# A two-block transformer step on one Trainium2 core: queries and keys projected by tokens, normed along the free axis, and turned by TensorE

## The chip, the cores and the metric

The kernel runs on 1 core of one Trainium2 chip, in one launch. The metric is the device time in microseconds. The kernel before takes 1256.78 us, the median of 3 runs (1255.48 to 1257.05). The trace comes from one further execution, of 1257.0 us, whose span from the first to the last instruction is 1253.6 us.

## What is computed

256 tokens of width 1024 go through two blocks, in float32.

Block one norms `x` and projects it with `w_in` into nine groups of columns. Three branches follow: a gated depthwise convolution over 31 taps with a layer norm; a differential attention with 8 heads, each with two maps of 64 dimensions; and a cross attention with 4 heads of 256 dimensions against a memory of 256 tokens. Queries and keys of both attentions are RMS-normed per head:

```
q = rms_norm(q.reshape(B, S, H, 2, d), qn_g)      # differential, d = 64
k = rms_norm(k.reshape(B, S, H, 2, d), kn_g)
q = rms_norm(q.reshape(B, S, X_HEADS, X_HEAD_DIM), qn_g)   # cross, 256
k = rms_norm(k.reshape(B, M, X_HEADS, X_HEAD_DIM), kn_g)
```

The three results are gated by the `merge` columns, summed, projected with `w_out` and added to `x`.

Block two norms again and runs a stick-breaking attention (8 heads of 64, normed queries `q2` and keys `k2`) beside a gated linear recurrence `h_t = a_t h_{t-1} + b_t` (`a_t` from a softplus of a constant `rg_lambda`). Then a layer picks, for each token and each of 8 heads, 16 of 16384 experts (two rows of 1024 each), and sums their outputs.

## The kernel before

**Slots and pieces.** Every projection is cut into slots of 512 output columns; a slot is two pieces, each 1 MB of weights (128 partitions x 2048 floats) loaded by one DMA of the SP queue. ScalarE (ACT) rounds a piece to `w_hi` (`hi`, L885), VectorE (DVE) forms the rest `w_lo` (`lo`, L1505), and TensorE (PE) makes three products for each tile: hi x hi (L443), input lo x w hi (L444), input hi x w lo (L445). Two raw buffers and three pairs of hi and lo buffers go round, so `hi` of piece p waits until TensorE is through with piece p-3.

**Two orientations.** In a channel-major slot the weights are stationary and 256 tokens move past: 4 x 8 tiles, 96 products of 256 columns, and the result lies by channels. In a token-major slot the input is stationary and 512 weight columns move: 8 x 2 tiles, 48 products of 512 columns, and the result lies by tokens. Queries and keys of both blocks are channel-major, values and merge columns token-major.

**A head norm before.** `head_copy` (L964) copies the slot out of PSUM and squares it on ACT; `head_sums` (L483) multiplies the squares by ones on TensorE, after the next slot's products; `head_root` (L1018) does a logarithm and an exponential over the spread sums on ACT, each with a table load (L876), since the two tables differ; `head_scale` (L1625) multiplies on DVE. In block two, `q2` and `k2` are first scaled by the token's inverse norm on DVE (`scale_slot`, L1618), which also empties PSUM.

**The order.** Each engine's program is written out by hand, and runs in that order. The attention loop goes over 18 slots: q0 k0 v0 q1 k1 v1 xq0 xq1 xk0 xk1 xv0 xv1 m0 to m5. In step n TensorE projects slot n, does the head sums of slot n-1, then work of attention heads: values of head n-5, transposes of the probabilities of head n-4, scores of head n-3 (the cross heads follow eight steps later). In step n DVE does `lo` of the piece two ahead, some convolution taps, the probabilities of head n-4, the second `lo`, taps again, the head scale, and the row maxima of head n-3. Taps on DVE: 3 after each `lo` for n under 4, 2 for n under 12, then 4. GpSimd (POOL) does tiles 3 to 6 of the convolution, and the last 8 of the 31 taps of tile 7, after DVE has done the first 23.

**After the attentions** come the slots dg0 dg1 xg0 xg1 dp0 dp1 cg0 cg1 xp0 xp1 cp0 cp1 o0 o1. The mean of the convolution's layer norm (`conv_mean`) is multiplied before dp0, its variance after dp0; DVE takes a reciprocal of the root (L2085) and does two operations for each of the 8 tiles. Then block two: the slots xr, q2, k2, g2, v2. Ahead of q2, ACT issues five DMAs (L1375, L1380), loads a table and computes `exp(-|lambda|)` (L1384, L1386), and DVE computes constants of the recurrence from it in a chain of small operations (L2154 to L2175) before `lo` of q2. The stick-breaking logits follow (`sb_logits`), then L621 (`sb_weights`), the output products, and the choice of experts. From the first choice on, POOL issues indirect DMAs that fetch an expert's two rows for each token.

## Time and profile before

| what | value |
|---|---|
| median of 3 runs | 1256.78 us |
| the profiled execution | 1257.0 us, span 1253.6 us |
| TensorE busy | 1109.1 us (88%) |
| VectorE busy | 976.4 us (78%) |
| ScalarE busy | 565.6 us (45%) |
| GpSimd busy | 564.7 us (45%) |
| mean DMA rate | 299 GB/s over the span |
| granted TensorE clock | 0.990 of full speed on average |

Busy time counts overlapping instructions once. Matmuls are pipelined: one is on record for longer than the distance to the next one's start, so a busy share of 1 does not say how fast the products follow each other; that is read from start times. The first half of the span, to about 606 us, is the two blocks' dense work; from there on the experts' rows are fetched, at about 427 GB/s.

### The profile page before, as it was taken

The page shows a single profiled execution, that of the slowest core. Times are in us where ns is not written, and L with a number is a line of the kernel's source. Part 1 is how long each engine was busy: PE and PEld are TensorE (multiplying, and loading weights), DVE is VectorE, ACT ScalarE, POOL GpSimd, SP SyncE. Part 2 cuts the span into 40 slices and gives each one's busy share as a digit, 9 for nine tenths or more (in the row PEclk, how much of TensorE's full clock was granted, in tenths as well). Part 3 has the DMA queues.
Part 4 walks back from the last instruction along what each step waited for, and adds up shares of the span by engine and source line. Part 5 has one row for each costly group of instructions (what it writes and reads, how often), then busy time and mean ns, then how long its engine had stood idle before and what let it go on. Part 6 is the DMA issues. An engine that isn't in the chain of part 4 may idle for free.

```text
span 1253.6 us, 14289 instructions
## 1 busy us (share of the span) xinstructions
PE 1109.1 (88%) x5044; PEld 747.1 (60%) x5044; DVE 976.4 (78%) x1972; ACT 565.6 (45%) x1037; POOL 564.7 (45%) x539
## 2 busy tenths in 40 slices
PE   6999999999999998999588987988878897788777
PEld 6989798788999888977343432444324443232222
DVE  5569989998789767687898678886788868787755
ACT  5666768764456444796323333233332333222311
POOL 0099999998320000000444554544544445343432
PEclk9999999999999999999899999999999999999999
DMA  6544333344555554335799999999999999999996
GB/s 245 202 169 158 132 144 139 137 148 153 202 189 181 205 194 171 145 123 227 308 427 427 426 427 427 427 426 427 428 426 427 427 426 424 427 427 423 427 426 272
DMA packets 53943, 374.27 MB, mean 299 GB/s; under 512 B 6896, under 2 KB 6896, under 8 KB 9200
## 3 DMA queue, kind: packets, MB, share of 16 engines
q0 software_dynamic: 37152, 268.45, 50.9%
q1 hardware_dynamic: 14512, 100.67, 22.1%
q10 hardware_dynamic: 2208, 4.24, 1.0%
q8 instruction: 39, 0.64, 0.2%
q14 instruction: 32, 0.26, 0.1%
HBM read 372.29 MB, written 1.05 MB: 298 GB/s over the span
## 4 chain that ended last, share of the span: by engine, by line
PE 44%; DMA 26%; DVE 21%; ACT 5%; issue 3%; POOL 0%; ACTq 0%; POOLq 0%; DVEq 0%; SPq 0%
DMA big<-in_experts,big 11%; PE unit L443 10%; PE unit L444 10%; PE unit L445 10%; PE unit L760 8%; DMA row<-in_experts,big 5%; DMA conv_in<-in_experts,big 5%; DMA work_two<-in_experts,big 4%; DVE w_lo L1505 3%; DVE row L1959 2%; DVE big L1959 2%; DVE big L1865 2%; ACT L876 2%; DVE big L1862 2%; DMA w_raw<-in_weights 1%
## 5 line engine op out<-in xcount | busy, mean ns | idle before, releaser
L1229 ACT ACTIVATE probs<-ident,big 128x128 f32<-128x128 f32 x255 | 102.4, 402 | 430.3 <-DVE big L1969 430.3
L443 PE MATMUL unit<-in_hi,w_hi 128*128 128x256 f32 x800 | 263.3, 329 | 3.9 <-DVE w_lo L1505 3.4
L760 PE MATMUL unit<-row,probs 128*128 128x512 f32 x448 | 215.3, 610 | 44.1 <-ACT probs L1229 43.9
L1505 DVE TENSOR_TENSOR w_lo<-w_raw,w_hi 128x2048 fp32r<-128x2048 f32 x89 | 205.9, 2319 | 54.8 <-ACT w_hi L885 54.5
L444 PE MATMUL unit<-in_lo,w_hi 128*128 128x256 f32 x800 | 226.9, 284 | 0.0
L445 PE MATMUL unit<-in_hi,w_lo 128*128 128x256 f32 x800 | 226.7, 283 | 0.0
L885 ACT CAST w_hi<-w_raw 128x2048 fp32r<-128x2048 f32 x89 | 169.1, 1905 | 96.8 <-PE unit L445 53.4
L760 PE MATMUL unit<-big,probs 128*128 128x512 f32 x344 | 168.4, 619 | 43.6 <-ACT probs L1229 43.5
L2333 POOL DMA_INDIRECT row<-in_experts,big x112 | 133.6, 1193 | 129.0 <-PE unit L760 113.3
L760 PEld LDWEIGHTS unit<-row,probs 128*128 128x128 f32 x448 | 78.2, 190 | 153.9 <-ACT probs L1229 95.3
L443 PEld LDWEIGHTS unit<-in_hi,w_hi 128*128 128x128 f32 x800 | 154.1, 193 | 26.6 <-issue 20.9
L444 PEld LDWEIGHTS unit<-in_lo,w_hi 128*128 128x128 f32 x800 | 154.2, 193 | 20.7 <-issue 20.6
L1959 DVE CUSTOM_DVE_ANT_0 row<-big,row 128x1024 f32<-128x1024 f32 x112 | 136.5, 1219 | 37.9 <-DMA row<-in_experts,big 37.9
L2333 POOL DMA_INDIRECT big<-in_experts,big x85 | 100.7, 1185 | 123.0 <-PE unit L760 108.7
L445 PEld LDWEIGHTS unit<-in_hi,w_lo 128*128 128x128 f32 x800 | 153.9, 192 | 0.0
L760 PEld LDWEIGHTS unit<-big,probs 128*128 128x128 f32 x344 | 60.7, 192 | 132.8 <-ACT probs L1229 87.2
L2314 POOL TENSOR_TENSOR conv_acc<-conv_acc,big 128x256 f32<-128x256 f32 x128 | 133.6, 1044 | 10.7
L1959 DVE CUSTOM_DVE_ANT_0 big<-big 128x1024 f32<-128x1024 f32 x87 | 106.1, 1219 | 35.8 <-DMA big<-in_experts,big 35.8
L2310 POOL TENSOR_SCALAR big<-conv_in,early_small 128x256 f32<-128x256 f32 x128 | 121.1, 946 | 24.6 <-DVE conv_acc L1528 23.9
L443 PE MATMUL unit<-w_hi,in_hi 128*128 128x512 f32 x304 | 120.5, 396 | 1.2 <-ACT work_one L984 1.2
L445 PE MATMUL unit<-w_lo,in_hi 128*128 128x512 f32 x304 | 118.4, 390 | 0.0
L444 PE MATMUL unit<-w_hi,in_lo 128*128 128x512 f32 x304 | 118.4, 389 | 0.0
(313 smaller groups left out, 1617.4 us busy)
## 6 DMA issues: line engine op xcount, KB each, us to landing
w_raw<-in_weights SPq DMA_DIRECT2D x90, 1024.0 KB, 4.8
w_waiting<-in_weights SPq DMA_DIRECT2D x2, 1024.0 KB, 8.1
row<-in_experts,big POOLq DMA_INDIRECT x112, 14.9
big<-in_experts,big POOLq DMA_INDIRECT x89, 13.4
big<-in_x SPq DMA_DIRECT2D x2, 512.0 KB, 5.4
big<-in_mem ACTq DMA_DIRECT2D x1, 1024.0 KB, 4.9
big<-in_x ACTq DMA_DIRECT2D x1, 1024.0 KB, 7.3
big<-in_sub_keys_t ACTq DMA_DIRECT2D x1, 1024.0 KB, 5.9
```

Of the source, the lines that this page charges most:

```text
L443: e.matmul(unit[:, to], *hi_hi, start=first, stop=False)
L444: e.matmul(unit[:, to], *hi_lo, start=False, stop=False)
L445: m = e.matmul(unit[:, to], *lo_hi, start=False, stop=final)
L760: m = e.matmul(unit[:, half * 512:(half + 1) * 512], diag_places[g % 12], UV.ap(g)[:, D + half * 512:D + (half + 1) * 512], start=first, s ...
L876: e.preload_act_table_set(sets[0])
L885: e.copy(split.ap(p)[0][:, :, :], raw.ap(p)[:, :, :]).then_inc(*mark("hi", p))
L1229: e.activation(diag_places[g % 12], ident[:, :], ACT.Copy, scale=here).then_inc(*mark("diag", g))
L1505: e.tensor_tensor(lo_part[:, :, :], raw.ap(p)[:, :, :], hi_part[:, :, :].bitcast(F32), ALU.subtract).then_inc(*mark("lo", p))
L1959: e.tensor_tensor_reduce(out=row_u, in0=h3[:, t, :], in1=row_u, scale=1.0, scalar=0.0, op0=ALU.mult, op1=ALU.add, accum_out=dot[t][:, n:n ...
L2310: e.tensor_scalar(product, src, tap, 1.0, ALU.mult, ALU.mult).then_inc(*mark("pool_product", (t, k)))
L2314: e.tensor_tensor(dst, dst, product, ALU.add).then_inc(*mark("pool_tap", None, *done))
L2333: e.indirect_dma_start(out=UV.ap(g), out_offset=None, in_=experts, in_offset=bass.IndirectOffsetOnAxis(ap=expert[t][:, n:n + 1], axis=0)). ...
```

## The change

Ten slots (q0 k0 q1 k1 xq0 xq1 xk0 xk1 q2 k2) become token-major. Their copy keeps tokens on partitions; squares are summed along the free axis (a DVE reduction for heads of 64, ACT's accumulator for heads of 256), the root is taken of 16 or 4 numbers for each token with one table that holds logarithm and exponential, DVE multiplies, TensorE transposes the eight 128 x 128 blocks (`head_turn`), and ACT applies the gain as it copies them out. The recurrence constants move ahead of the first slot. The taps' schedule, the shared tile, the order around the layer norm, and block two's PSUM places change as well.

```diff
-SHARED_TILE, SHARED_TAPS = 7, 23
+SHARED_TILE, SHARED_TAPS = 7, 19
...
-        add_slots("x", (f"q{i}", "w_in", COL_Q + i * SLOT), (f"k{i}", "w_in", COL_K + i * SLOT))
-        add_slots("x", (f"v{i}", "w_in", COL_V + i * SLOT), token_major=True)
-    add_slots("x", *((f"xq{i}", "w_in", COL_XQ + i * SLOT) for i in range(2)))
-    add_slots("mem", *((f"xk{i}", "w_mem_kv", i * SLOT) for i in range(2)))
+        add_slots("x", (f"q{i}", "w_in", COL_Q + i * SLOT), (f"k{i}", "w_in", COL_K + i * SLOT),
+                  (f"v{i}", "w_in", COL_V + i * SLOT), token_major=True)
+    add_slots("x", *((f"xq{i}", "w_in", COL_XQ + i * SLOT) for i in range(2)),
+              token_major=True)
+    add_slots("mem", *((f"xk{i}", "w_mem_kv", i * SLOT) for i in range(2)),
+              token_major=True)
...
+    add_slots("b2", ("q2", "w_in_2", 0), ("k2", "w_in_2", D_SB), token_major=True)
...
# TensorE
+            def head_turn(name, place=None):
+                src, unit = tm_half(HEAD_NORMS[name][0]), units.take(name + " turn", place)
+                for wait in W(("scaled heads", name), units.free(name + " turn")):
+                    e.wait_ge(*wait)
+                for j in range(4):
+                    for t in range(TT):
+                        to = j * T + t * P
+                        m = e.transpose(unit[:, to:to + P], src[:, t, j * P:(j + 1) * P],
+                                        ident[:, :])
+                m.then_inc(*mark("turned heads", name))
...
-                if pending in HEAD_NORMS:
+                if pending in BY_TOKENS:
+                    head_turn(pending)
...
+            project(slot["dp0"])
             conv_mean()
-            project(slot["dp0"])
+            project(slot["dp1"])
             conv_variance()
-            for name in ("dp1", "cg0", "cg1", "xp0", "xp1"):
+            for name in ("cg0", "cg1", "xp0", "xp1"):
...
             half_project(slot["g2"], 0, 0)
-            head_sums("q2", 1)
-            head_sums("k2", 2)
             half_project(slot["g2"], 1)
-            half_project(slot["v2"], 0, 2)
+            head_turn("q2", 1)
+            head_turn("k2", 2)
+            half_project(slot["v2"], 0, 0)
             sb_logits("A", 1)
-            sb_logits("B0", 0)
+            sb_logits("B0", 2)
# ScalarE
+            def head_copy_by_tokens(name):
+                dst = tm_half(HEAD_NORMS[name][0])
...
+                if name in ("q2", "k2"):
...
+                    for t in range(TT):
+                        a = e.activation(dst[:, t, :], tm(units.ap(name))[:, t, :], ACT.Copy,
+                                         scale=inv_rms["b2"][1][:, t:t + 1])
+                else:
+                    a = e.copy(dst, tm(units.ap(name)))
...
+                if dim == DIFF_HEAD_DIM:
+                    e.activation(work.ap(name)[:, :], flat(HEAD_NORMS[name][0]),
+                                 ACT.Square).then_inc(*mark("sq", name))
+                    return
...
+                        a = e.activation(work.ap(name)[:, i * dim:(i + 1) * dim], dst[:, t, c],
+                                         ACT.Square, accum_out=head_rms[:, i:i + 1])
...
+            def head_roots_by_tokens(name):
+                table(LN_EXP)
...
+                e.activation(head_rms, head_rms, ACT.Ln, bias=EPS6,
+                             scale=1.0 / HEAD_NORMS[name][3]).then_inc(*mark("ln", name))
...
+                e.activation(head_rms, head_rms, ACT.Exp, scale=-0.5).then_inc(
+                    *mark("root", name))
...
+            def head_gains(name):
...
+                for j in range(per_head):
+                    a = e.activation(dst[:, j:4:per_head, :], unit[:, j:4:per_head, :], ACT.Copy,
+                                     scale=gain[:, j:j + 1])
...
+                if pending in BY_TOKENS:
+                    exps.insert(0, partial(head_roots_by_tokens, pending))
                 ahead(s, between=exps)
-                if name in HEAD_NORMS:
+                if name in BY_TOKENS:
+                    head_copy_by_tokens(name)
...
+                if pending in BY_TOKENS:
+                    head_gains(pending)
# after dp1's first piece; before, one slot earlier, with Sqrt and a DVE reciprocal
+            hi(slot["dp1"].pieces[1] + 2)
+            hi(slot["cg0"].pieces[0] + 2)
+            table(LN_EXP)
...
+            e.activation(rs, units.ap("variance")[:, 0:T], ACT.Ln, bias=EPS5, ...)
+            e.activation(rs, rs, ACT.Exp, scale=-0.5).then_inc(*mark("root", "rs"))
+            table(EXP_TANH)
+            hi(slot["cg0"].pieces[1] + 2)
+            for half in range(2):
+                for k in range(4 * half, 4 * half + 4):
+                    e.activation(conv_acc[:, k, :], conv_acc[:, k, :], ACT.Identity,
+                                 bias=v("conv_ln_b", k), scale=0.25)...
+                conv_silu(half)
# VectorE
+            def head_squares_by_tokens(name):
+                dim = HEAD_NORMS[name][3]
+                if dim == DIFF_HEAD_DIM:
...
+                    e.tensor_reduce(rms_of(name),
+                                    work.ap(name)[:, :].rearrange("p (i c) -> p i c", c=dim),
+                                    AX, ALU.add)...
+            def head_scale_by_tokens(name):
...
+                e.tensor_tensor(dst, dst, head_rms.unsqueeze(2).to_broadcast(
+                    [P, 4 * T // dim, dim]), ALU.mult).then_inc(*mark("scaled heads", name))
...
+                if pending in BY_TOKENS:
+                    head_squares_by_tokens(pending)
+                    norms.insert(0, partial(head_scale_by_tokens, pending))
-                ahead(s, between=norms, convolve=3 if n < 4 else 2 if n < 12 else 4)
+                ahead(s, between=norms, convolve=3 if n < 4 else 1 if n < 10 else 4)
```

Also: the two small ACT operations and the DVE chain of the recurrence constants, with the table load, stand right after the gains, before the first slot; the four DMAs of `rg_w_a` and `rg_w_x` are issued right after `tile_squares_b2(0)`, and the one of the keys after the copy of `b2_inv`; the clearing of their target stands in DVE's work for o1. On DVE, `conv_sum` moves behind the first `lo` of dp0's step, the subtraction of the mean behind the branch of dp0, `square_sum` into dp1's step, the scaling of the 8 tiles (one operation each) into cg0's. In block two DVE's order is: `q2` reduced after `lo` of k2, `k2` reduced before `drive`, both multiplied after the scan.

## Rows read from the trace of the kernel before

**Rows 1.** Windows: us, busy (instructions) of PE, PEld, DVE, ACT, POOL; clock, DMA share, GB/s

```profile
61.00:319.00 258.00, 253.85 (x1527) 222.21 (x1526) 230.25 (x263) 170.17 (x218) 234.65 (x243) 1.00 0.43 150
319.00:480.00 161.00, 160.49 (x995) 144.87 (x994) 126.66 (x115) 77.63 (x66) 19.79 (x16) 1.00 0.54 194
...
606.00:1254.00 648.00, 524.03 (x1368) 228.16 (x1368) 496.58 (x1399) 195.79 (x596) 301.12 (x258) 0.98 0.99 416
```

**Rows 2.** Waits of TensorE from 20 to 480 us: us in total, times, longest

```profile
PE bank L529 <- DVE probs L1686: 2.9, 4, 1.6
PE unit L443 <- ACT work_one L984: 1.2, 1, 1.2
```

**Rows 3.** Timeline of TensorE, steps of k1 and v1: start us, us, instructions

```profile
114.28 0.39 PE L443 MATMUL unit<-in_hi,w_hi 128*128 128x256 f32 x1
...
125.89 1.88 PE L491 MATMUL unit<-work_two,ones 128*128 128x512 f32 x4
127.61 0.49 PE L529 MATMUL bank<-ident,probs 128*128 128x128 f32 x3
...
128.89 0.50 PE L443 MATMUL unit<-w_hi,in_hi 128*128 128x512 f32 x1
...
139.94 1.88 PE L491 MATMUL unit<-work_one,ones 128*128 128x512 f32 x4
```

**Rows 4.** Groups by form up to 560 us: busy us, mean ns; idle before, releasers

```profile
L443 PE MATMUL unit<-in_hi,w_hi 128*128 128x256 f32 x704 | 202.7, 288 | 3.9 <-DVE w_lo L1505 3.4 <-DVE in_lo L1592 0.5
...
L443 PE MATMUL unit<-w_hi,in_hi 128*128 128x512 f32 x304 | 120.5, 396 | 1.2 <-ACT work_one L984 1.2
```

**Rows 5.** Chain of waits, start us, us: sums of a 256-wide head; eight transposes

```profile
171.68 1.73 PE unit L497 x8
...
448.83 0.88 PE unit L474 x8
```

**Rows 6.** Groups of VectorE by form, 61 to 319 us (columns as in rows 4)

```profile
L1505 DVE TENSOR_TENSOR w_lo<-w_raw,w_hi 128x2048 fp32r<-128x2048 f32 x37 | 86.9, 2348 | 11.9 <-ACT w_hi L885 11.8
L1528 DVE SCALAR_TENSOR_TENSOR conv_acc<-conv_in,early_small,conv_acc 128x256 f32<-128x256 f32 x99 | 73.3, 785 | 0.2
...
L1662 DVE TENSOR_REDUCE col<-probs 128x2 f32<-128x512 f32 x8 | 5.5, 688 | 0.3
```

**Rows 7.** Groups of ScalarE by form, 61 to 319 us (columns as in rows 4)

```profile
L885 ACT CAST w_hi<-w_raw 128x2048 fp32r<-128x2048 f32 x36 | 68.5, 1908 | 19.4 <-PE unit L445 16.0 <-DMA w_raw<-in_weights 3.4
L876 ACT ACT_TABLE_LOAD x21 | 26.9, 1283 | 0.4
...
L976 ACT ACTIVATE work_two<-big 128x1024 f32<-128x1024 f32 x5 | 5.3, 1058 | 0.2
```

**Rows 8.** Timeline of VectorE between 400 and 541 us

```profile
405.93 4.49 DVE L1505 TENSOR_TENSOR w_lo<-w_raw,w_hi 128x2048 fp32r<-128x2048 f32 x2
...
490.15 0.17 DVE L2154 TENSOR_SCALAR col<-col 128x4 f32<-128x4 f32 x1 [5.17 <-ACT col L1386]
...
493.27 4.49 DVE L1505 TENSOR_TENSOR w_lo<-w_raw,w_hi 128x2048 fp32r<-128x2048 f32 x2
...
533.42 2.44 DVE L2226 TENSOR_TENSOR_SCAN big<-conv_acc,big 128x256 f32<-128x256 f32 x4
537.90 1.28 DVE L1632 SCALAR_TENSOR_TENSOR big<-big,col,work_two 128x1024 f32<-128x1024 f32 x1 [2.04 <-ACT work_two L1004]
```

**Rows 9.** Timeline of TensorE between 410 and 556 us

```profile
410.56 0.40 PE L443 MATMUL unit<-w_hi,in_hi 128*128 128x512 f32 x1
...
491.96 0.60 PE L659 MATMUL bank<-work_one,ones 128*128 128x256 f32 x2
495.61 0.58 PE L443 MATMUL unit<-in_hi,w_hi 128*128 128x256 f32 x1 [3.05 <-DVE w_lo L1505]
...
553.82 1.95 PE L621 MATMUL unit<-work_one,later 128*128 128x512 f32 x4 [0.94 <-issue]
```

**Rows 10.** Window (columns as in rows 1) right after the wait before q2

```profile
495.00:499.00 4.00, 3.39 (x16) 3.39 (x17) 3.96 (x5) 0.00 (x0) 0.00 (x0) 0.57 0.56 195
```

## What the change does to the time, predicted before it was run

> **What bounds the kernel now.** I read the windows first, then TensorE's waits, its timeline, and the groups of the other engines. The span has two halves. From 606 us on the DMA share is 0.99 [rows 1]: that half moves a fixed number of bytes and starts with the first choice of experts, so whatever ends earlier in front of it moves the end by the same amount. The dense half is bound by TensorE: from 61 to 319 us (q0 to m5) it is busy 253.9 of 258 us, from 319 to 480 us 160.5 of 161 [rows 1], and all its waits from 20 to 480 us that the view names are small, 2.9 us for the probabilities of attention heads and 1.2 us for a PSUM unit that a head's sums still hold [rows 2]. VectorE is close behind: 230 of the 258 us [rows 1]. ScalarE has room (170).
>
> So two questions decide: how much shorter TensorE's own stream gets, and where VectorE or ScalarE is then late.
>
> **How fast products follow each other.** k1, channel-major, runs from 114.28 to 125.89: 96 products in 11.61 us, 0.121 each. v1, token-major, runs from 128.89 to 139.94: 48 products in 11.05 us, 0.230 each [rows 3]. A turned slot saves 0.56 us. The records' own durations, 288 and 396 ns [rows 4], overlap and are no pace.
>
> Here a rule of the Trainium skill speaks for more: TensorE: Matmul & The Clock Gate, section Back-to-back issue gap, gives a sustained spacing of about 131 ns for 512 columns in a stream of weight loads and matmuls. By it a token-major slot would take an estimated 6.3 us and ten slots would save over 50. The trace has 230 ns for such a pair, in float32 parts, so the sum goes by the trace.
>
> **Attention stage, 61 to 319 us.** Eight slots turn.
> - Slots: 8 x 0.56 = 4.5 us less.
> - Head sums go: 125.89 to 127.61 is 1.72 us [rows 3], 1.73 for a 256-wide head [rows 5]. Eight transposes come, 0.88 us [rows 5]: 8 x 0.85 = 6.8 us less. Float32 transposes from other tiles could differ; bounds 0.8 to 1.7 us each.
> - The unit wait in front of v0 (1.2 us) ended with a logarithm behind two ACT operations and a table load. Its successor ends with the gain copy, behind two operations of about 1.06 [rows 7]. About 0.5 us stays: 0.7 less.
> - VectorE. Added: a reduction of 1024 columns for the four slots with 64-wide heads. 512 columns take 0.69 [rows 6], so 1.2 to 1.4; I take 1.2 (bounds 0.7, as if it ran twice as fast, and 2.35, what 2048 columns cost in `lo`). The multiply by a broadcast root takes half a `lo`, 1.2 (bounds 0.7 and 1.5); 8 of them are 9.8 us, in place of scales that took 1.3 to 1.5 for q and k and two of 1.06 for xq and xk, 14 us. Taps in the loop go from 104 to 100, 3.1 us less [rows 6]. Net 4.8 - 4.4 - 3.1 = -2.7: some 228 us of work in a stage that shrinks to about 247. On average VectorE still fits. But the steps are uneven: the taps fall to 2 a step for n = 4 to 9 (TensorE's step 13.7 us, VectorE's 13 to 14), and rise from 4 to 8 a step in n = 10 and 11, 3.1 us more each, where TensorE's step is now 1.4 us shorter. There VectorE needs 17.5 and 16.3 us against 13.7. Laid end to end with these durations, the probabilities are late by 1.9 and 1.5 us at those two steps, 0.5 at the next, and 0.7 once for k0's multiply, about 4.9 in all. The same list for the kernel as it is gives about 3.9 for the waits of rows 2 with their issue time. So 1.0 more.
> - ScalarE loses two table loads of 1.28 for each head slot [rows 7] and two 1024-column operations become 16 numbers wide; it gains a gain copy, and for 256-wide heads four squares with sums instead of one, about 1 us more. Net about 3 us less a slot, all beside TensorE: worth nothing but slack.
>
> Sum: -4.5 - 6.8 - 0.7 + 1.0 = -11.0 us, bounds -12.5 (no late probabilities) and -7.4 (reduction 1.5, multiply 1.8).
>
> **The constants.** Ahead of the first slot VectorE waits for its second raw piece, with nothing to do for the 3.1 us that the chain takes (490.15 to 493.27 [rows 8]): 0, bounds 0 and +1.
>
> **Layer norm, 319 to 480 us.** TensorE's stream keeps its length. The shared tile now has 12 taps on POOL instead of 8; 8 took 19.8 us busy [rows 1], so 12 take about 30, from the same point in dg0's step on, and `conv_sum` needs them only in dp0's, 38 us later: hidden. What is late is the first piece of xp0. Before, `lo` for xp0's first piece ran 405.93 to 408.2, for a start at 410.56 [rows 8, 9]: 2.4 us of slack. After, the norm's last part begins one slot later, at the end E of dp1. ScalarE: `hi` 1.9, two table loads 2.6, logarithm and exponential 0.9, `hi` again at E+7.9 (it waits for half of cg0), eight adds and two tanh of 256 and 1024 columns 5.5, the split of xg 2.2, cg0's tanh 1.0: E+17. VectorE: its half of the split ends at E+17.8, then 2.3 for the two products with the tanh, 2.5 for cg0's gate, 2.2 for `lo`: E+25. xp0 could start at E + 0.24 + 2 x 11.5 = E+23.2. TensorE waits 1.9 us; bounds 0 and 4. These lengths are estimates from 1.06 us for 1024 columns on ScalarE and 2.35 for 2048 on VectorE [rows 6, 7]. Sum: +1.9.
>
> **Block two, 480 to 554 us.**
> - The wait before q2 goes. TensorE stands from 491.96 to 495.61 for `lo` of q2, which waits for the chain, which waited 5.17 us for ScalarE's DMAs, table load and two small operations [rows 8, 9]. Without them `hi` and `lo` of q2 end by about 491: 3.4 us less. Behind that wait the granted clock was 0.57 on average over 4 us [rows 10]; q2 took 13.0 us, not 11.6: 1.4 less. The rg DMAs move to a place where ScalarE waited for TensorE's transposes: 0.
> - q2 and k2 turned: 2 x 0.56 = 1.1 less. Their sums, four products of 512 columns with the time that TensorE waits between them, 3.4 us, become two transposes and a gap, 2.1: 1.3 less. TensorE also stood 0.9 us and a semaphore in front of L621 [rows 9], for ScalarE's logarithms; these come earlier: 1.1 less.
> - What is late next: `head_turn("q2")`. Before, q2's norm had until the logits, behind half of v2. Now it stands ahead of v2, and the multiply stands behind the scan on VectorE. From xr's end at 491.96: q2 to 503.2, gate and k2 to 517.3, g2 to 528.9. ScalarE does the copy of k2 and its square after `hi` of v2, to 522.7; VectorE reduces to 523.9, then drive 1.2, `lo` 2.3, product 1.3, scan 2.4 [rows 8], multiply 1.2: 532.3. TensorE waits 3.4 us (bounds 1 and 6). By what the wait before q2 did, this one should bring a stretch at half clock too: another 1.2 (bounds 0 and 1.5).
>
> TensorE then reaches L621 at about 550.2, where it was at 553.82 [rows 9]: -3.4 - 1.4 - 1.1 - 1.3 - 1.1 + 3.4 + 1.2 = -3.7. ScalarE, which limits next, starts the stick-breaking logarithms about 4 us earlier, so it doesn't take this back. Bounds -7 and 0.
>
> **After 554 us** TensorE's products follow without a break until the first scores, and nothing there changes: the shift is carried.
>
> **Sum.** -11.0 + 1.9 - 3.7 = -12.8 us on the profiled execution, 1257.0 to 1244.2. That execution lies 0.2 above the median, so 1244.0.
>
> **The rivals.**
> - *VectorE becomes the bound (slower).* The place is the attention stage, the price the reductions and the broadcast multiplies. The rule of the Trainium skill in VectorE: DVE Perf Modes, section Rules for kernel authors, speaks for it: a reduction on a hot path is the slowest kind of operation, and should be restructured away. The row has 688 ns for 512 columns, the pace of `lo`. With 2.0 for the reduction and 2.5 for the multiply my list has the stage's gain at 2.2 us instead of 11.0; with both at about 2.7, more than twice the rows, the whole gain is gone and beyond it the kernel is slower: about 1260. For it: 230 of 258 us busy. Against: every 1024-column row costs 1.2 to 1.5. Chance 0.07.
> - *The new waits take most back.* Late probabilities, xp0 and `head_turn("q2")` at their upper ends: -7.4 + 4 + 0 = -3.4, 1253.4. For it: three places where my margin is under 2 us. Chance 0.17.
> - *The pace is that of the records.* If wide products really cost 396 against 288 ns, ten slots would fall by 8 us each: about 1180. Rows 3 are against it. Chance 0.01.
> - *The start of the second half is held by something else* (a buffer, a weight load), and nothing arrives at the end: 1257. Against: TensorE runs without a break up to the first scores. Chance 0.03.
> - *The forecast*, within 4 us of 1244: chance 0.72.
>
> **Numbers.** The range runs from 1238.5 (waits at their lower ends: -12.5, 0, -6) to 1252 (into the second rival). A measurement of this kernel tells 0.2%, 2.5 us, from no change. Faster by more than that: the forecast and most of the second rival, 0.88. Within: 0.05, the rest of the second and the held start. Slower: 0.07.
>
> **What would show it.** Right: token-major head slots of about 11.05 us on TensorE and transposes of about 0.9; m5 ending near 308 us; ACT table loads between q0 and m5 down from 21 to a handful; no wait before q2; a wait of some 3 us before the transposes of q2, followed by a clock below 1; L621 near 541 us (553.8 less 12.8). Wrong: TensorE waiting for probabilities in most steps from v1 on with VectorE near 100% busy; a wait at dp0 for POOL's taps; a wait above 4 us at xp0 or at the transposes of q2; or an unchanged distance from the first gather to the end not holding (648 us).

## The result, and the profile after

The changed kernel takes 1239.26 us, the median of 4 runs (1238.69 to 1240.34), beside 1256.9 for the kernel before: a ratio of 0.9865, 95% interval 0.9851 to 0.9879. The forecast was 1244.0, with a range from 1238.5 to 1252: the sign and the range hold, and the gain is 17.6 us where 12.8 were forecast. The result lies 0.8 us from the lower end of the range, and not all of the surplus was earned (see below).

The profiled execution takes 1239.2 us, with a span of 1237.0. Windows of the changed kernel, first the attention stage, then the layer norm's stage, block two up to the suffix sums, the second half, and four microseconds soon after the new wait, which ends at 518.93 (columns as in [rows 1]):

```profile
60.40:305.30 244.90, 241.91 (x1155) 199.16 (x1154) 230.58 (x257) 151.44 (x242) 232.85 (x230) 1.00 0.45 157
305.30:467.10 161.80, 161.22 (x997) 145.25 (x996) 129.43 (x109) 81.51 (x75) 45.34 (x38) 1.00 0.55 195
467.10:536.80 69.70, 66.97 (x408) 59.37 (x407) 49.77 (x59) 52.77 (x65) 0.00 (x0) 0.98 0.42 155
602.00:1237.00 635.00, 518.22 (x1356) 224.14 (x1355) 484.22 (x1358) 188.60 (x585) 292.51 (x250) 1.00 0.99 419
520.00:524.00 4.00, 3.96 (x16) 3.46 (x16) 3.34 (x3) 3.19 (x3) 0.00 (x0) 0.57 0.00 0
```

VectorE did as much in the attention stage as before (230 us), in 13 us less. The other thing to see is the first number behind the comma, TensorE's: 3.0 us of the 244.9 are without a matmul.

The timeline of TensorE gives the borders of the stages (start us, length us): q0's first product, the transposes of k0 between two slots, the first products of dg0, xp0, xr and q2, the transposes of q2 and k2, the suffix sums.

```profile
60.42 0.40 PE L455 MATMUL unit<-w_hi,in_hi 128*128 128x512 f32 x1
...
96.66 1.04 PE L521 MATMUL unit<-ident,big 128*128 128x128 f32 x8
97.46 0.48 PE L455 MATMUL unit<-w_hi,in_hi 128*128 128x512 f32 x1
...
305.28 0.28 PE L455 MATMUL unit<-in_hi,w_hi 128*128 128x256 f32 x1
...
397.31 0.50 PE L455 MATMUL unit<-w_hi,in_hi 128*128 128x512 f32 x1
...
467.12 0.36 PE L455 MATMUL unit<-in_hi,w_hi 128*128 128x256 f32 x1
...
478.87 0.60 PE L683 MATMUL bank<-work_one,ones 128*128 128x256 f32 x2
479.12 0.58 PE L455 MATMUL unit<-w_hi,in_hi 128*128 128x512 f32 x1
...
518.93 2.95 PE L521 MATMUL unit<-ident,big 128*128 128x128 f32 x16 [2.69 <-DVE big L1750]
...
536.83 0.59 PE L645 MATMUL unit<-work_one,later 128*128 128x512 f32 x1
```

The same borders of the kernel before, read from start times in its trace, are 61.23, 318.75, 410.56, 480.22 and 553.82 us (q0 there is channel-major like the slots ahead of it; its first product is the 192nd before the sums at 84.28). So the 16.6 us by which the span is shorter come about like this:

| stretch | before | after | difference | forecast |
|---|---|---|---|---|
| to q0 | 61.23 | 60.42 | -0.8 | 0 |
| q0 to m5 | 257.52 | 244.86 | -12.7 | -11.0 |
| dg0 to xr | 161.47 | 161.84 | +0.4 | +1.9 |
| xr to the suffix sums | 73.60 | 69.71 | -3.9 | -3.7 |
| suffix sums to the end | 699.8 | 700.2 | +0.4 | 0 |
| outside the span | 3.4 | 2.2 | -1.2 | 0 |

The last row is probably scatter: in other executions of the kernel before, what lies around the span is 2.0 to 3.9 us, in the four of the changed kernel 2.1 to 2.2.

Waits of TensorE in the attention stage of the changed kernel, which answer to [rows 2]; and the waits of VectorE there, then those of the kernel before (61 to 319 us), each with us in total, times and longest:

```profile
PE bank L553 <- DVE probs L1801: 2.2, 3, 1.3
PE unit L455 <- ACT big L1056: 0.7, 1, 0.7
```

```profile
DVE w_lo L1601 <- ACT w_hi L912: 11.5, 9, 2.9
```

```profile
DVE big L1632 <- ACT work_two L994: 6.9, 4, 2.7
DVE big L1632 <- ACT work_one L994: 5.6, 1, 5.6
```

The first is the wait for rounded weights, which was 11.8 before. L1632 is the head scale: before, it waited 12.5 us for roots; its successor, the multiply L1750, waits for none in this stage. Groups by form of the changed kernel, 60 to 305 us (columns as in [rows 6]), show what VectorE paid:

```profile
L1750 DVE TENSOR_TENSOR big<-big,col 128x1024 f32<-128x1024 f32 x8 | 11.9, 1485 | 0.0
...
L1739 DVE TENSOR_REDUCE col<-work_one 128x16 f32<-128x1024 f32 x2 | 2.4, 1214 | 0.3 <-ACT work_one L1025 0.3
```

ScalarE's table loads in the stage are 6 where [rows 7] have 21:

```profile
L903 ACT ACT_TABLE_LOAD x6 | 7.7, 1283 | 0.1
```

### The profile page after: what moved, and what is told of

It is laid out like the page before. It is cut to its first block, busy times and chain, and to the rows that moved or that the text cites. A ratio compares the mean times of both kernels' runs of the same rounds, so it can differ in the third digit from the quotient of the medians.

```text
span 1237.0 us, 13405 instructions
## 1 busy us (share of the span) xinstructions
PE 1090.6 (88%) x4588; PEld 717.2 (58%) x4588; DVE 979.2 (79%) x1960; ACT 550.1 (44%) x1075; POOL 590.6 (48%) x547
## 4 chain that ended last, share of the span: by engine, by line
PE 42%; DMA 25%; DVE 24%; ACT 5%; issue 3%; POOL 0%; POOLq 0%; DVEq 0%; SPq 0%; ACTq 0%
DMA big<-in_experts,big 11%; PE unit L455 9%; PE unit L456 9%; PE unit L457 9%; PE unit L784 9%; DMA conv_in<-in_experts,big 5%; DMA work_two<-in_experts,big 4%; DMA row<-in_experts,big 4%; DVE w_lo L1601 3%; DVE row L2074 2%; DVE big L2074 2%; DVE big L1980 2%; DVE conv_acc L1624 2%; DVE big L1977 2%; DVE big L2084 1%
## 5 line engine op out<-in xcount | busy, mean ns | idle before, releaser
L455 PE MATMUL unit<-w_hi,in_hi 128*128 128x512 f32 x464 | 184.7, 398 | 0.7 <-ACT big L1056 0.7
L456 PE MATMUL unit<-w_hi,in_lo 128*128 128x512 f32 x464 | 181.1, 390 | 0.0
L457 PE MATMUL unit<-w_lo,in_hi 128*128 128x512 f32 x464 | 181.0, 390 | 0.0
L455 PE MATMUL unit<-in_hi,w_hi 128*128 128x256 f32 x480 | 170.1, 354 | 1.5 <-DVE in_lo L1688 1.3
L2427 POOL TENSOR_TENSOR conv_acc<-conv_acc,big 128x256 f32<-128x256 f32 x132 | 143.6, 1088 | 11.0
L2423 POOL TENSOR_SCALAR big<-conv_in,early_small 128x256 f32<-128x256 f32 x132 | 135.3, 1025 | 3.5 <-DVE conv_acc L1624 2.5
L456 PE MATMUL unit<-in_lo,w_hi 128*128 128x256 f32 x480 | 135.6, 283 | 0.0
L457 PE MATMUL unit<-in_hi,w_lo 128*128 128x256 f32 x480 | 135.5, 282 | 0.0
L455 PEld LDWEIGHTS unit<-in_hi,w_hi 128*128 128x128 f32 x480 | 91.8, 191 | 22.4 <-issue 20.7
L456 PEld LDWEIGHTS unit<-in_lo,w_hi 128*128 128x128 f32 x480 | 91.9, 191 | 20.2 <-issue 20.1
```

The source lines that it names most:

```text
L455: e.matmul(unit[:, to], *hi_hi, start=first, stop=False)
L456: e.matmul(unit[:, to], *hi_lo, start=False, stop=False)
L457: m = e.matmul(unit[:, to], *lo_hi, start=False, stop=final)
L2423: e.tensor_scalar(product, src, tap, 1.0, ALU.mult, ALU.mult).then_inc(*mark("pool_product", (t, k)))
L2427: e.tensor_tensor(dst, dst, product, ALU.add).then_inc(*mark("pool_tap", None, *done))
```

## Experiments

Ratios are to the kernel before, run beside each kernel on the same chip; the changed kernel itself has 0.9865 (0.9851 to 0.9879). 0.001 is 1.26 us. Differences to the changed kernel are worked out from the ratios; by the medians alone they come out up to 1.1 us otherwise (0.3 for e6's 1.4, 2.1 for e4's 3, 5.5 for e2's 6.1). Each ratio has an interval of about 0.0013 to either side, unless given.

### The constants alone, and the constants put back

```diff
# e1: kernel before
+            (ScalarE: |lambda|, exp behind the exponentials of lambda; VectorE: the chain ahead of the first slot)
-            (both in front of q2; ScalarE's five DMAs moved as in the change)
# e2: changed kernel, the same edit undone
```

> The kernel before, with one part of the change: the recurrence constants are worked out ahead of the first slot, and the DMAs that ScalarE issued in front of q2 move as in the changed kernel. Slots, sums, taps and the layer norm stay. Theory (the wait before q2 was worth its length and the clock behind it): TensorE's 3.65 us between xr and q2 fall to 0.25, q2 itself takes 11.6 instead of 13.0 us, and all of it arrives: 1256.9 - 3.4 - 1.4 = 1252.1 us. Rival (ScalarE's logarithms for the stick-breaking limit anyway): the wait in front of the suffix sums (1.33 us before) grows by what q2 gained, and the time is 1255 to 1257. It also prices the chain at its new place: TensorE's products start at 13.1 us from the span's start as before if it is free there, up to 1 us later if not.

> The changed kernel, with the recurrence constants and ScalarE's DMAs put back in front of q2. Theory: the wait before q2 is there again with 3.4 us, q2 loses another 1.4 to 2 us to a clock at half, and nothing later takes it up, since the wait before the transposes of q2 hangs on TensorE's own gates and moves with them: 1239.3 + 5.1 = 1244.4 us. Rival (one wait covers for the other): with VectorE's chain for k2 and the scan in the same place in time, the 2.96 us wait before the transposes shrinks by what q2 comes later, and the kernel loses 2 us or less, 1241.

Measured: e1 1250.72 us, 0.9964 (0.9951 to 0.9978), so 4.6 us less; e2 1244.77 us, 0.9914, so 6.1 us more than the changed kernel. In e1 the wait is gone and q2 runs at full clock; q2's first product in the timeline of its TensorE (xr ends at 491.16), and the window that answers to [rows 10]:

```profile
491.41 0.47 PE L443 MATMUL unit<-in_hi,w_hi 128*128 128x256 f32 x1
```

```profile
495.00:499.00 4.00, 4.00 (x35) 4.00 (x35) 4.00 (x11) 1.40 (x1) 0.00 (x0) 1.00 0.71 270
```

Between xr's start and the suffix sums e1 takes 68.92 us (479.42 to 548.34), 4.7 less than before: 3.4 of wait, 1.3 of clock. In e2 both waits stand side by side:

```profile
PE unit L455 <- DVE w_lo L1604: 4.0, 1, 4.0
PE unit L521 <- DVE big L1753: 2.7, 1, 2.7
```

So the wait before q2 was worth its length and the clock, nothing took it back, and the new wait doesn't hang on it. The expectations were 1252.1 (a ratio of 0.9962) and 1244.4 us. More than a quarter of the change's gain is this part, which has nothing to do with the orientation. e1's TensorE also begins at 12.99 us as before (13.08): the chain costs nothing at its new place.

### What holds the transposes of q2 and k2

```diff
# e3: changed kernel, VectorE
             lo(piece("v2", 0))
+            head_scale_by_tokens("q2"); head_scale_by_tokens("k2")
             (drive, scan)
-            head_scale_by_tokens("q2"); head_scale_by_tokens("k2")
# e5: as e3, and scale_slot("g2", ...) ahead of drive and scan too
# e4: changed kernel, TensorE
             half_project(slot["g2"], 1)
+            half_project(slot["v2"], 0, 2)
             head_turn("q2", 1)
-            head_turn("k2", 2)
-            half_project(slot["v2"], 0, 0)
+            head_turn("k2", 0)
...          (the PSUM places of what follows swapped to suit)
```

> The changed kernel; on VectorE the two multiplies of q2 and k2 by their roots go ahead of the last product of the drive and the scan. Theory: the wait of 2.96 us before the transposes of q2 has its place in that order alone. VectorE stood idle for 2.07 us in front of the product, both roots are there by 514.3 us, so the multiplies end by 516.8 and TensorE, through with g2 at 516.0, waits 0 to 0.3 us; the stretch at half clock behind the wait (3.4 us long, costing 2.0) goes too: -4.7 us, 1234.6. Rival (the scan is as urgent): g2's scaling on VectorE, the gelu and the exponentials on ScalarE are late in its place, TensorE waits in front of the suffix sums, and 2 us or more are given back: 1236.5 to 1239.

> The changed kernel; on TensorE the transposes of q2 and k2 go behind the first half of v2 (5.5 us), with PSUM places to suit, VectorE's order as in the changed kernel. Theory: the half slot covers the 2.96 us wait and there is no stretch at half clock behind it (2.0), but the gain copies of ScalarE now stand right in front of the logits: TensorE waits 1 to 1.5 us there. 1239.3 - 2.96 - 2.0 + 1.3 = 1235.6. Rival (what counts is when ScalarE gets the logits): its table load, gelu and casts end at the same time as before and the suffix sums wait for its exponentials: no gain beyond 2 us, 1237.5 to 1239.5.

> As the kernel with the multiplies first, and VectorE's scaling of g2 too goes ahead of the drive and the scan. With the multiplies alone first, TensorE's transposes began at 515.5 us without a wait, but v2 then stood 3.3 us for g2's PSUM unit, which that scaling empties behind the scan (520.7 us). Theory (the 2.96 us wait had two ends within 0.4 us of each other, the multiply and g2's unit; with both gone it is gone): the scaling ends by 517.0, v2 follows the transposes at 517.4, and what is late next is ScalarE's chain of gelu, casts, table load and three operations of the first logits: it starts when logits or rg output arrive and ends about 530.4, with VectorE's two operations behind it by 532.9, where the suffix sums start at 536.6 now. So 3.6 us less than the changed kernel, a ratio to the kernel before of about 0.9836. Rival (ScalarE's and VectorE's chain does not move, since the scan is 3.5 us later in it): the suffix sums start at 536 again and the ratio is 0.986 to 0.987.

Measured: e3 1239.07 us, 0.987 (0.9855 to 0.9885): no gain, so the rival's size, but g2's scaling held up v2 and not the suffix sums. e4 1241.31 us, 0.989 (0.9874 to 0.9905): the rival, and beyond it, some 3 us above the changed kernel by the ratios. e5 1235.21 us, 0.9838 (0.9825 to 0.9852), as expected to 0.3 us.

Timeline of e3's TensorE (the transposes run from 515.53 without a wait, which has moved to the instruction behind them), then of VectorE in e3 and in e5:

```profile
520.72 0.70 PE L455 MATMUL unit<-w_hi,in_hi 128*128 128x512 f32 x1 [3.29 <-DVE big L1718]
```

```profile
513.50 2.35 DVE L1750 TENSOR_TENSOR big<-big,col 128x1024 f32<-128x1024 f32 x2
515.77 1.22 DVE L2338 SCALAR_TENSOR_TENSOR big<-big 128x1024 f32<-128x1024 f32 x1
517.02 2.44 DVE L2342 TENSOR_TENSOR_SCAN big<-conv_acc,big 128x256 f32<-128x256 f32 x4
519.38 1.20 DVE L1718 TENSOR_TENSOR big<-unit,work_one 128x1024 f32<-128x1024 f32 x1
```

```profile
513.60 2.35 DVE L1750 TENSOR_TENSOR big<-big,col 128x1024 f32<-128x1024 f32 x2
515.87 1.22 DVE L1718 TENSOR_TENSOR big<-unit,work_one 128x1024 f32<-128x1024 f32 x1
```

v2 needs the PSUM unit that `scale_slot("g2")` (L1718) empties. In the changed kernel that ends at 521.15, just before the transposes are through (521.53), so the list of waits names the multiply alone; e3 takes the multiply away and finds the other end. e5 takes both away: v2 follows at 517.28, and no stretch of low clock comes. What is left is a wait of 1.3 us in front of the suffix sums, for ScalarE's three operations on the first logits and VectorE's two behind them, which end at 532.88:

```profile
PE unit L645 <- issue: 1.3, 1, 1.3
```

In e4 TensorE does useful work in place of the wait, but ScalarE then stands 6.6 us for the transposes, its operations on the first logits run from 531.2 us (changed: 530.1), and TensorE stands 4.55 us in front of the suffix sums with a low clock behind it:

```profile
537.08 3.46 PE L645 MATMUL unit<-work_one,later 128*128 128x512 f32 x4 [4.55 <-issue]
```

### How full VectorE is

```diff
# e7: changed kernel, in head_scale_by_tokens, block one only
+                for _ in range(2):
+                    e.tensor_scalar(dst, dst, 1.0, None, ALU.mult).then_inc(*mark("again"))
+                    e.wait_ge(*at(now("again"))[1:])
# e6: changed kernel, taps
-                convolve=3 if n < 4 else 1 if n < 10 else 4)
+                convolve=3 if n < 4 else 2 if n < 12 else 4)
# e11: kernel e5, taps
+                convolve=3 if n < 4 else 1 if n < 10 else 2 if n < 12 else 4 if n < 16 else 6)
```

> The changed kernel with two more operations of VectorE for each of the eight head slots of block one, ahead of the multiply by the root: a multiplication of its 1024 columns by 1, which changes nothing (0.7 us each by the 1024-column row of a plain scaling, 1.46 with the semaphores, 11.7 us over the stage). Theory (VectorE has 14 us of room in the stage as a whole, but its steps from k0 to v1 are 94 to 100% busy): TensorE loses 4 to 7 us, by waits for probabilities and for turned heads; ratio 0.990 to 0.992. Rival one (VectorE is the bound already): all 11.7 us arrive, 0.996. Rival two (there is room in each step, since each operand is prepared a slot ahead): 0 to 1 us, 0.987.

> The changed kernel with the taps of VectorE spread as in the kernel before: 3 after each first operand for n under 4, 2 for n under 12, then 4 (changed: 1 from n = 4 to 9, then 4). The taps of the shared tile stay at 19 on VectorE. Theory (VectorE's steps of n = 4 to 9 are full, 12.6 to 14.2 us busy of TensorE's 13.0 to 14.4): two more taps (1.55 us) in each of these six steps make TensorE wait 4 to 6 us there, and the waits for probabilities at n = 10 to 12 (2.5 us above the issue time in the changed kernel) go: +2 to +3 us, a ratio of 0.988 to 0.989. Rival (only the sum over the stage counts, 230 of 245 us): no new waits, the 2.5 us go: 0.9845.

> The kernel with multiplies and g2 first, and VectorE's taps moved from the steps n = 10 and 11 (4 to 2 behind each first operand) to n = 16 and 17 (4 to 6), where VectorE is busy 9.8 of 12.5 and 9.5 of 11.1 us. Theory (the waits at n = 10 to 12 are the 3.1 us of taps that stand between the first operand and the probabilities): those waits, 0.72 + 1.44 + 0.31 us above their issue time, go, and nothing comes in their place: -2.2 to -2.5 us on the kernel with multiplies and g2 first (0.9838), ratio 0.982. Rival (VectorE's work is only put off, as when two taps a step were spread over n = 4 to 11, where the sum of the waits stayed): 0 to -1, 0.983 to 0.984.

Measured: e7 1253.37 us, 0.9979 (0.997 to 0.9988), 14.3 us more than the changed kernel. Its added rows, and TensorE's waits of 60 to 320 us:

```profile
L1751 DVE TENSOR_SCALAR big<-big 128x1024 f32<-128x1024 f32 x16 | 15.4, 964 | 0.3
...
L1753 DVE TENSOR_TENSOR big<-big,col 128x1024 f32<-128x1024 f32 x8 | 13.1, 1634 | 0.3
```

```profile
PE bank L553 <- DVE probs L1804: 8.3, 7, 1.8
PE unit L521 <- DVE big L1753: 6.8, 4, 2.9
```

VectorE works 16.6 us more (15.4, and 1.2 in the multiplies). TensorE waits 15.1 us for it by these two rows and not 2.2, and the stage is 14.9 us longer (60.07 to 319.85): nine tenths arrive, a clock of 0.65 over 4 us behind the wait of 2.9 included. My 4 to 7 us counted on 14 us of room, which is there on average but not where it is needed; rival one was right. e6, 1239.6 us and 0.9876, lies 1.4 us above the changed kernel, inside the intervals of both; in the trace its stage is 245.45 us, 0.6 more. The waits at n = 10 to 12 go and others come at n = 4, 5 and 8: neither +2 to +3 nor a gain. Its profiled execution is the fastest of its four, which run from 1237.7 to 1240.7, and it shows why one trace of such a kernel is not enough: the new wait before the transposes of q2 is there, and this time the clock stays at 1.00 behind it.

```profile
519.18 2.23 PE L521 MATMUL unit<-ident,big 128*128 128x128 f32 x16 [2.80 <-DVE big L1750]
```

```profile
519.20:523.20 4.00, 3.82 (x23) 3.12 (x24) 4.00 (x3) 2.85 (x3) 0.00 (x0) 1.00 0.00 0
```

e11, 1233.17 us and 0.9821 (0.9808 to 0.9834), takes the same waits away and brings none in the stage, since n = 16 and 17 had room: its stage is 242.2 us (59.93 to 302.11), 2.7 less than the changed kernel's and 2.6 less than e5's. But between dg0 and xr it takes 162.6 us and not 161.8, with two small waits for second operands (0.28 and 0.23 us), so 0.8 come back there and the kernel gains 2.0 us on e5: a part of the rival, that the work is only put off.

```profile
PE bank L553 <- DVE probs L1801: 0.3, 1, 0.3
```

### Where a head's norm stands

```diff
# e8: changed kernel
-        BY_TOKENS = ("q0", "k0", "q1", "k1", "xq0", "xq1", "xk0", "xk1", "q2", "k2")
+        BY_TOKENS = ("q0", "k0", "q1", "k1", "q2", "k2")
+        (token_major=True goes from xq0, xq1, xk0, xk1)
# e9: changed kernel, head_roots_by_tokens, block one only
+                    table(SQRT)
                 table(LN_EXP)
```

> The changed kernel with the four slots of the cross attention (xq0 xq1 xk0 xk1) by channels, normed as in the kernel before; the other six stay by tokens. Theory (a slot is worth 0.57 us by its orientation and 0.86 by eight transposes in place of eight products for the sums): four slots, 5.7 us back, and VectorE's multiply is 0.6 us longer for each, which shows as up to 1 us of waits for probabilities: +5.7 to +6.7, ratio 0.991 to 0.992. ScalarE's table loads (two more for each of the four) cost nothing. Rival (the gain of a slot lies with ScalarE's table loads and its longer norm, not with TensorE's own stream): much less or much more than 5.7, and with other waits than for probabilities. Rival (wide products cost the 396 to 288 ns of the records): 32 us back, slower than the kernel before.

> The changed kernel with two more table loads of ScalarE (another table and back, 2.57 us) in front of each root of the eight head slots of block one; nothing else. In the changed kernel VectorE never waits for a root in this stage; in the kernel before it waited 12.5 us for roots there (rows of its waits, 5 times), and 12.1 us in the kernel with the cross heads by channels, where the waits for probabilities doubled. Theory (ScalarE's shorter norm paid a part of the gain: it is what lets VectorE carry the reductions and multiplies): the loads put the root 2.6 us later, VectorE stands 1 to 2.5 us at its multiply in most of the eight steps, and TensorE waits for probabilities: +4 to +9 us on the changed kernel, ratio 0.990 to 0.994. Rival, as forecast (ScalarE has 90 us of room, its table loads are worth nothing): within 1 us of the changed kernel, 0.986 to 0.987.

Measured: e8 1247.55 us, 0.9938 (0.9924 to 0.9952), 9.2 us more than the changed kernel; e9 1239.19 us, 0.9863, no difference that the interval separates; in its trace the attention stage is 0.9 us longer (245.7), with the wait for probabilities at n = 10 at 1.3 us in place of 0.6. In e8 each slot takes 11.61 us and each head's sums 1.73, where the changed kernel has 11.04 and 0.87: the 5.7 us expected. The other 3.5 us are waits for probabilities, most of them at two steps, where the changed kernel waits 0.55 and 1.28:

```profile
211.64 0.55 PE L551 MATMUL bank<-ident,probs 128*128 128x128 f32 x3 [1.80 <-DVE probs L1799]
229.53 0.55 PE L551 MATMUL bank<-ident,probs 128*128 128x128 f32 x3 [3.02 <-DVE probs L1799]
```

Before them VectorE stands for roots. Its timeline in e8, and ScalarE's, from which the root comes:

```profile
198.90 1.70 DVE L1726 SCALAR_TENSOR_TENSOR big<-big,early_small,work_one 128x512 f32<-128x512 f32 x2 [2.88 <-ACT work_one L1074]
```

```profile
192.82 1.01 ACT L993 COPY big<-unit 128x1024 f32<-128x1024 f32 x1 [1.79 <-PE unit L455]
...
196.23 0.69 ACT L1064 ACTIVATE work_one<-unit,col 128x512 f32<-128x512 f32 x1
198.23 0.63 ACT L1074 ACTIVATE work_one<-work_one 128x512 f32<-128x512 f32 x1
```

By channels the root stands behind the copy and the square of the next slot, so at the end of a step; by tokens it stands between the two pieces, half a slot earlier. There even 21 table loads in place of 6 (e9, the count in its groups) make VectorE wait for no root. My theory for e9 blamed the loads and fell; what helped is the place, as far as e8 and e9 tell: that is argued from them, not shown. A kernel with the norm by tokens and its root at the old place wasn't run.

### The layer norm's chain

```diff
# e10: changed kernel, ScalarE, conv_silu
+                for _ in range(2):
+                    (the same tanh into the same tile, and a wait for it)
                 e.activation(..., ACT.Tanh, scale=2.0).then_inc(*mark("tanh", f"z{half}"))
```

> The changed kernel; each of the two tanh of the convolution's gate on ScalarE is done three times over (4 x 1.06 us and semaphores more, about 4.5 us), which changes no value. Theory (the chain of the layer norm ends just in time: the second operand of xp0's first piece starts on VectorE at 394.97 us and ends 0.1 us before TensorE is through with cg1): nearly all of it arrives as a wait before xp0, 4.3 us, with up to 1.5 us for a clock at half behind it: ratio 0.990 to 0.991. Rival (there is still the slack of about 2 us that the kernel before has): 2.3 us and 0.988 to 0.989.

Measured: 1244.62 us, 0.9908 (0.9893 to 0.9923), 5.4 us more, at the upper end of the theory; the wait is there in full, with a low clock behind it (window 402 to 406):

```profile
401.60 0.53 PE L455 MATMUL unit<-w_hi,in_hi 128*128 128x512 f32 x1 [4.43 <-DVE w_lo L1605]
```

```profile
402.00:406.00 4.00, 4.00 (x12) 3.18 (x11) 3.97 (x3) 0.00 (x0) 0.00 (x0) 0.58 0.82 291
```

The chain has no slack left in the changed kernel, where it had 2.4 us before.

### The best version

```diff
# e12: kernel e11, ScalarE and VectorE
+            sb_logs("A")
             mix_hi(4, rg_gain, slice(0, T), [("rg out", None)], "rg")
-            sb_logs("A")
...
+            sb_log_weights("A")
             mix_lo(4, rg_gain, slice(0, T), "rg")
-            sb_log_weights("A")
```

> As the kernel with the late taps, and ScalarE does the three operations of the first stick-breaking logits ahead of the cast of the recurrence's output, VectorE its two operations of them ahead of the lower part of that output. Theory (with multiplies and g2 first TensorE waits 1.4 us and an issue time in front of the suffix sums, for this chain, which stands 1.7 us of cast and 1.1 us of idle time later than it could): the wait goes, -1.4 us, ratio 0.981. Rival (the recurrence's output is then what is late, in the output products 6 us behind, or the second logits are): no gain, 0.982.

Measured: 1232.57 us, 0.9815 (0.9802 to 0.9828). The wait in front of the suffix sums is gone, but 0.5 us come back within them; the step over e11 is 0.6 us (expected 1.4), which the intervals don't separate. Against the changed kernel e12 is 6.3 us faster and computes the same.

## Why the forecast was right, and where it was short

- **The pace.** Products of 512 columns follow each other by 0.227 to 0.230 us, 11.04 us a slot, against 0.121 for 256 columns. Forecast 8 x 0.56, measured 5.0 us (q0 and k0 took 23.05 together by channels and 21.8 by tokens, and q1 by channels had 0.4 of a gap). The 0.131 us that TensorE: Matmul & The Clock Gate, section Back-to-back issue gap, of the Trainium skill has for such a pair shows nowhere in these runs.
- **Sums into transposes.** Forecast 6.8; eight heads took 13.4 us and take 7.0, so 6.4: k0's sums had been 1.3, not 1.7.
- **The unit wait** before v0: 0.7 forecast, 0.6 measured.
- **Late probabilities.** This term had the wrong sign: +1.0 forecast, -0.7 measured. In front of the transposes of probabilities TensorE's last instruction and the wait take 5.5 us before and 4.75 after, of which 1.8 in both are issue. At n = 10 and 11, where I had 1.9 and 1.5, 0.7 and 1.4 came; at n = 12 0.3 for 0.5; k0's multiply, 0.7 forecast, delays nothing. The reduction was sized right (1.21 for 1.2), the multiply too short (1.49 for 1.2); eight multiplies at 1.2 are 9.6 and not the 9.8 written there, and the net of -2.7 uses 9.6.
- **VectorE as the bound** was given 0.07. The mechanism is nearer than that: e7 has the gain nearly used up (0.9979) with two operations of 0.96 us more a head. My list had it gone at about 2.7 us for each of the two new kinds, 1.5 and 1.2 above what they cost; that agrees. The rule in VectorE: DVE Perf Modes, section Rules for kernel authors (Trainium skill), to restructure a reduction on a hot path, has as its reason that a reduction is the slowest operation, and that isn't borne out here: the reduction of 1024 columns takes 1.21 us, the pace of the 512-column row (688 ns) and of `lo`, and the multiply takes longer. What e7 bears out is that added work on this engine arrives, of whatever kind.
- **ScalarE's savings.** "Worth nothing but slack" holds for the table loads within 1 us (e9). That the root moves half a slot earlier was not weighed at all.
- **The constants at their place**: 0, as e1 shows. The 0.8 us by which q0 starts earlier are not theirs: q0 starts at 60.19 us in e2, which has the constants at the old place. Of that, 0.5 is there when TensorE starts (8.95 us for 9.44), the rest is in small waits before q0. In the twelve experiments q0 starts between 59.9 and 60.4 us, with 60.40 in e1, so the one trace of the kernel before may be a late one. The cause is open.
- **Layer norm.** The wait of 1.9 us at xp0 didn't come. ScalarE's `hi` that waits for half of cg0 began at E + 6.4 us (E, the end of dp1, is 373.6 us), not E + 7.9, and the split of xg ended on VectorE at E + 16.7, not E + 17.8; the second operand was ready at E + 23.6, and TensorE could have used it at E + 23.5: xp0's first product starts 0.35 us after the last of cg1 and not 0.12. So the place had no slack left, which e10 shows, and cost 0.2 us, half of the 0.4 in the table. POOL's 12 taps were hidden.
- **Block two.** -3.7 forecast, -3.9 measured, and its parts hold: the wait before q2 3.4 (e1), clock 1.3, the new wait 2.96 for 3.4. The clock behind the new wait cost 1.3 us for 1.2: transposes and v2's half take 2.6 and 6.6 us, and 2.4 and 5.5 in e6's execution, which has the same wait and a clock of 1.00. In e5 the transposes take 1.7, since there they don't stand for k2's multiply either.
- **Carried on** behind 554: within 0.4 us.

The mechanism of the forecast holds: shorter slots, sums that become transposes, and the wait before q2 gone, each near its price. The term that was most off is the late probabilities (1.7 us of the 5.0 by which the profiled execution is faster than forecast), then xp0 (1.5). The start (0.8) and what lies around the span (1.2) belong to no step of the change that is known, and no view could have given them; without these two the time would have been 1241.3, so that part of the surplus is luck. The range's lower end counts -6 for block two, whose own bound was -7; with it the range would begin a microsecond lower, which changes nothing here.

## What to carry to other kernels

A wait has as many ends as it has late producers: before moving the one that the trace names, list when the others end, since the next may be 0.4 us behind (e3 gained nothing, e5 3.4 us). Room on an engine counts step by step: 14 us of idle VectorE in a stage covered 1.7 of 16.6 us of added work, while eight taps moved to steps with real room gave 2.6 us in the stage and 2.0 in the kernel, since what is moved late reaches into the next stage. And a producer's place in another engine's program can matter more than its length, so read where the consumer stands for it before pricing what is saved there.

## What the runs showed of the hardware

Between q0 and the suffix sums the fourteen traces have fourteen places where TensorE stood idle for 2.7 to 4.6 us (the idle time before an instruction, as the timeline gives it). Behind twelve of them the granted clock over the next 4 us was 0.57 to 0.67, with stretches at 0.50, the lower of the two levels (1.2 of 2.4 GHz): before q2 in the kernel before, before the transposes of q2 in the changed kernel and most others, before v2 in e3, before xp0 in e10, before the suffix sums in e4, in the attention stage of e7. Behind two it stayed at 1.00: 2.80 us before the transposes in e6, and 3.02 us in e8's attention stage. Behind no wait of up to 1.8 us did it fall. What decides between the twelve and the two isn't shown. Where the clock fell, it cost 1.3 us before q2 (against e1) and before the transposes (against e6), and 1.6 us in e3 (v2's half, 7.15 for 5.55) and in e4 (from the suffix sums to the products behind them, 3.6 for 2.05). So a wait of 3 us is worth 4 to 5, as e1 measures (3.4 of wait, 4.7 in all), but not in every execution.

VectorE's multiply of 1024 columns took 1.21 us four times and 1.76 us four times in the attention stage, where GpSimd is busy 95%, and 1.20 and 1.22 in block two, where GpSimd is idle. SBUF — State Buffer, section SBUF: two separate sides, of the Trainium skill says that VectorE and GpSimd share a pair of ports which one instruction holds to its end, and that a VectorE operation with two SBUF inputs can be held up by it. The start times bear this out: each of the four long ones, and each of the five long ones of e5, began 0.11 us after a GpSimd operation with two inputs from SBUF had started (0.79 us, so 0.67 were left, and 0.55 is what the multiply lost); each of the short ones, four and three, began while a GpSimd scaling ran, which then took 1.70 us, where most of them take 0.5 to 0.7. The same slot (k0) is long in the changed kernel and short in e5, so the shape of the tile doesn't decide it. No run here took GpSimd's work away, so the cause is strongly suggested but not shown.
